# First norm of a two-layer diffusion backbone: modulation, norm and first products taken one input tile at a time

## The reference

```python
def rms(x):
    xf = x.astype(jnp.float32)
    return (xf * lax.rsqrt(jnp.mean(xf * xf, axis=-1, keepdims=True) + EPS)).astype(x.dtype)

def modulate(x, shift, scale):
    return rms(x) * (1 + scale[:, None]) + shift[:, None]
...
    mod = jax.nn.silu(c) @ p['w_ada'] + p['b_ada']
    mod_c = (jax.nn.silu(c_ctx) @ p['w_ada'] + p['b_ada'])[None]
    sh1, sc1, g1, sh2, sc2, g2 = jnp.split(mod, 6, axis=-1)
...
    h = modulate(x, sh1, sc1)
    hc = modulate(cx, csh1, csc1)
    z = h @ p['w_in']
```

## Time and profile before

| | us |
|---|---|
| median of 3 runs (lowest, highest) | 2370.47 (2367.01, 2371.37) |
| the profiled execution: its time | 2370.61 |
| its span in the profile | 2368.9 |
| PE busy | 2278.4 (96%) |
| DVE busy | 1348.6 (57%) |
| ACT busy | 937.4 (40%) |
| POOL busy | 164.8 (7%) |
| granted clock of PE, mean | 0.992 |

### The profile page before, as it was taken

The page is one execution under the profiler, slowest core; times in us unless marked ns, Lnnn a source line. Parts: engine busy times, 40 slices in busy tenths (PEclk is TensorE's granted clock), DMA queues, the critical chain, the costliest instruction groups (busy, mean ns, idle before and its releaser), DMA issues.

```text
span 2368.9 us, 35088 instructions
## 1 busy us (share of the span) xinstructions
PE 2278.4 (96%) x12916; PEld 1896.0 (80%) x12916; DVE 1348.6 (57%) x1954; ACT 937.4 (40%) x1381; POOL 164.8 (7%) x169
## 2 busy tenths in 40 slices
PE   6999988999999999999999999999999998999999
PEld 6788766788888878888888876776788878888887
DVE  6555566476667475425534566556745566645545
ACT  3454556522223243213312345546643334423332
POOL 2113010000000000000000002220100000000000
PEclk9999999999999999999999999999999999999999
DMA  7112110244343311111111131121045552222223
GB/s 284 45 54 72 36 40 19 72 156 138 133 142 133 124 54 62 62 63 63 62 62 63 62 117 63 63 71 32 36 144 176 175 178 78 101 98 92 94 98 115
DMA packets 58625, 221.26 MB, mean 93 GB/s; under 512 B 6720, under 2 KB 6720, under 8 KB 57872
## 3 DMA queue, kind: packets, MB, share of 16 engines
q1 hardware_dynamic: 44496, 160.46, 19.5%
q0 software_dynamic: 14016, 59.26, 7.1%
HBM read 214.45 MB, written 5.24 MB: 93 GB/s over the span
## 4 chain that ended last, share of the span: by engine, by line
PE 86%; DVE 6%; ACT 3%; issue 3%; DMA 1%; PEldq 0%; SPq 0%; PEld 0%; DVEq 0%; ACTq 0%
PE PS L611 83%; PE PS L903 3%; DVE TM L1459 1%; ACT W_hi L1081 1%; DVE XY L1459 1%; ACT TM L1081 1%; DVE H_lo L1459 1%; DVE ROPE L1512 1%; DVE W_lo L1456 1%; ACT XY L1081 1%; DVE F_lo L1456 1%; DMA ROPE<-w_mod 1%; ACT F_hi L1081 0%; DMA XY<-x_in 0%; ACT H_hi L1081 0%
## 5 line engine op out<-in xcount | busy, mean ns | idle before, releaser
L611 PE MATMUL PS<-H_hi,W_hi 128*128 128x512 f32 (+1 forms) x2256 | 689.3, 358 | 25.0 <-DVE H_lo L1459 9.6
L611 PE MATMUL PS<-H_hi,W_lo 128*128 128x512 f32 (+1 forms) x2256 | 678.7, 354 | 0.0
L611 PE MATMUL PS<-H_lo,W_hi 128*128 128x512 f32 (+1 forms) x2256 | 676.3, 353 | 0.0
L1456 DVE TENSOR_TENSOR W_lo<-W_st,W_hi 128x1024 fp32r<-128x1024 f32 x278 | 343.5, 1237 | 569.3 <-ACT W_hi L1081 567.8
L1081 ACT ACTIVATE W_hi<-W_st 128x1024 fp32r<-128x1024 f32 x278 | 293.7, 1057 | 838.8 <-PE PS L611 829.1
L611 PEld LDWEIGHTS PS<-H_hi,W_hi 128*128 128x128 f32 x2256 | 377.1, 189 | 102.9 <-issue 30.5
L611 PEld LDWEIGHTS PS<-H_lo,W_hi 128*128 128x128 f32 x2256 | 374.5, 189 | 61.3 <-issue 2.7
L611 PEld LDWEIGHTS PS<-H_hi,W_lo 128*128 128x128 f32 x2256 | 375.2, 189 | 59.1
L611 PE MATMUL PS<-F_hi,W_hi 128*128 128x512 f32 (+1 forms) x968 | 296.2, 355 | 13.5 <-DVE XY L1459 5.1
L611 PE MATMUL PS<-F_hi,W_lo 128*128 128x512 f32 (+1 forms) x968 | 295.3, 354 | 0.0
L611 PE MATMUL PS<-F_lo,W_hi 128*128 128x512 f32 (+1 forms) x968 | 293.3, 352 | 0.0
(11 more groups left out here) (129 smaller groups left out, 2086.9 us busy)
## 6 DMA issues: line engine op xcount, KB each, us to landing
W_st<-w_all SPq DMA_DIRECT2D x278, 512.0 KB, 3.5
RA<-w_mod POOLq DMA_DIRECT2D x40, 512.0 KB, 3.7
TM<-w_mod POOLq DMA_DIRECT2D x40, 512.0 KB, 3.7
RA<-w_ada SPq DMA_DIRECT2D x8, 512.0 KB, 8.7
XY<-bias_na POOLq DMA_DIRECT2D x2, 1792.0 KB, 7.3
RA<-w_mod SPq DMA_DIRECT2D x6, 512.0 KB, 8.2
XY<-x_in SPq DMA_DIRECT2D x4, 768.0 KB, 11.5
x_spill<-XY POOLq DMA_DIRECT2D x1, 3072.0 KB, 11.1
```

The source lines that it names most:

```text
L611: return nc.tensor.matmul(o, lhsT, rhs, start=start, stop=stop)
L1456: return nc.vector.tensor_tensor(o, a, b, f)
```

## The change

In layer 0 alone, the modulation, the norm and the first two output tiles of the input stage are interleaved over the eight input tiles.

- SP's order of loads is a list, FIRST_LOADS: scale and x first, W blocks 0 and 1 after x piece 2, the shift tiles from place 12 on.
- PE: the sum of squares is eight accumulated products of the squares with the matrix of 1/1024, over all 768 columns. The shift of tile j is a row: the conditioning columns are now stationary (128x2), the weight tile moves (128 columns, eight k). ACT copies the row (2x128) to SBUF, PE turns it into a column (128x2) by a product with a 2x2 identity, DVE adds the bias. Then, for each k, PE makes shift row k+2, shift column k+1, and the products of input tile k with W blocks 0 and 1.
- POOL's six additions go.
- ACT: six squares, both W_hi, two squares, the root over 768 columns, two copied rows, and per k the two pieces of H_hi and the copy of row k+2.
- DVE: scale sums 0 to 2, both W_lo, sums 3 and 4, the scale of five tiles, the Newton step over 768 columns, and per k the shift addition, both products, H_lo of tile k-1, and the scale sums of tile k+5 with its three small steps.
- The early tiles are inside PE's first_norm, ahead of its phase marks; `two_early_tiles` stays for the other norms.

```diff
+def first_norm_counts():
+
+    return dict(sq=KT, y0=1, y_sq=1, newton=2, norm_u=2 * KT, norm_hi=2 * KT, norm_lo=2 * KT)
+
+
+FIRST_LOADS = (("scale", 0), ("x", 0), ("scale", 1), ("x", 1), ("scale", 2), ("x", 2), ("w", 0), ("w", 1), ("x", 3),
+               ("scale", 3), ("scale", 4), ("shift", 0), ("shift", 1), ("shift", 2), ("scale", 5), ("shift", 3),
+               ("scale", 6), ("shift", 4), ("scale", 7), ("shift", 5), ("shift", 6), ("shift", 7))
+AHEAD = 5

...
-            for j in range(KT):
-                if j >= 3:
-                    sp.wait_ge(S["scale_acc"], 2 * (j - 2))
-                sp.dma_start(SCALE_W[j % 3], w_mod[SC1 + j]).then_inc(scale_loaded[j % 3], 16)
-                if j >= 3:
-                    sp.wait_ge(S["ada_used"], j - 2)
-                sp.dma_start(SHIFT_W[j % 3], w_ada[j]).then_inc(shift_loaded[j % 3], 16)
-                if j < KT // 2:
+            for what, j in FIRST_LOADS:
+                if what == "scale":
+                    if j >= 3:
+                        sp.wait_ge(S["scale_acc"], 2 * (j - 2))
+                    sp.dma_start(SCALE_W[j % 3], w_mod[SC1 + j]).then_inc(scale_loaded[j % 3], 16)
+                elif what == "shift":
+                    if j >= 3:
+                        sp.wait_ge(S["ada_used"], j - 2)
+                    sp.dma_start(SHIFT_W[j % 3], w_ada[j]).then_inc(shift_loaded[j % 3], 16)
+                elif what == "x":
                     k = 2 * T * j
                     sp.dma_start(XY[:, k:k + 2 * T], x_in[:, k:k + 2 * T]).then_inc(x_loaded[j], 16)
+                else:
+                    sp.dma_start(W_st[:, j, :], w_all[IN_BLOCKS[j]]).then_inc(w_loaded[j], 16)
             for l in range(DEPTH):
                 b0 = B_LAYER * l
                 for v, stored in enumerate(IN_BLOCKS):
-                    load(b0 + v, (b0 + v) % 2, B_LAYER_STORED * l + stored, first=b0 + v < 2)
+                    if b0 + v >= 2:
...
             pool.dma_start(PAR[:, :], par[0]).then_inc(S["par_loaded"], 16)
-            for k in range(1, KT - 1):
-                pool.wait_ge(S["sq"], k + 1)
-                wait(pool, "sq_sum", k - 1)
-                nc.gpsimd.tensor_tensor(TT, SQ[0] if k == 1 else TT, SQ[k % 2], ALU.add).then_inc(S["sq_sum"], 1)
             pool.wait_ge(S["scale_acc"], 2 * KT)
...
-            def ada_tile(o, w):
+            def shift_rows(j):
+
+                pe.wait_ge(shift_loaded[j % 3], 16 * (j // 3 + 1))
+                wait(pe, "sh_row", j - 1)
                 for k in range(KT):
-                    ins = mm(o, w[:, P * k:P * k + P], CC[:, k, :], k == 0, k == KT - 1)
-                return ins
-
-            def ada():
-
-                pe.wait_ge(S["silu_c"], 1)
-                for j in range(KT):
-                    pe.wait_ge(shift_loaded[j % 3], 16 * (j // 3 + 1))
-                    ada_tile(PS[:, 2 * j:2 * j + 2], SHIFT_W[j % 3]).then_inc(S["ada_used"], 1)
+                    ins = mm(bank(4 + j % 2)[0:2, 0:P], CC[:, k, :], SHIFT_W[j % 3][:, P * k:P * k + P], k == 0,
+                             k == KT - 1)
+                ins.then_inc(S["ada_used"], 1)
+
+            def shift_columns(j):
+
+                pe.wait_ge(S["sh_row"], j + 1)
+                pe.wait_ge(S["newton"], 1)
+                wait(pe, "sh_add", j - 1)
+                mm(bank(6 + j % 2)[:, 0:2], SH_ROW[j % 2], MT[0:2, M_ID, 0:2], True, True).then_inc(S["sh_tr"], 1)

...
             def first_norm():
-                pe.wait_ge(S["sq_sum"], KT - 2)
-                for h, (s0, sn) in enumerate(halves(T)):
-                    mm(stat_at(T, h), MT[:, M_ONE, :], TT[:, s0:s0 + sn], True, False)
-                pe.wait_ge(S["sq"], KT)
-                for h, (s0, sn) in enumerate(halves(T)):
-                    mm(stat_at(T, h), MT[:, M_ONE, :], SQ[1][:, s0:s0 + sn], False, True).then_inc(S["ss"], 1)
-                base.advance(**norm_counts(False))
+                pe.wait_ge(S["const_loaded"], 16)
+                for k in range(KT):
+                    pe.wait_ge(S["sq"], k + 1)
+                    for s0, sn in segs(T):
+                        ins = mm(pair(3)[:, s0:s0 + sn], MT[:, M_ONE, :], SQ[k % 2][:, s0:s0 + sn], k == 0, k == KT - 1)
+                    ins.then_inc(S["sq_pass"], 1)
+                pe.wait_ge(S["silu_c"], 1)
+                shift_rows(0)
+                shift_rows(1)
+                shift_columns(0)
+                for k in range(KT):
+                    if k + 2 < KT:
+                        shift_rows(k + 2)
+                    if k + 1 < KT:
+                        shift_columns(k + 1)
+                    for t in range(2):
+                        if k == 0:
+                            have_block(t)
+                        pe.wait_ge(S["norm_hi"], 2 * k + 2)
+                        pe.wait_ge(S["norm_lo"], 2 * k + 2)
+                        ins = gemm_k(t, T, t, k, KT, H_hi, H_lo)
+                        if k == KT - 1:
+                            ins.then_inc(S["block_done"], 1)
+                base.advance(**first_norm_counts())

...
-                    act.wait_ge(x_loaded[k // 2], 16)
-                    wait(act, "sq_sum", k - 1 if k >= 2 else 0)
-                    op(SQ[k % 2][:, 0:w], X3[:, k, 0:w], ACT.Square).then_inc(S["sq"], 1)
-                for b in range(2):
-                    split_hi(b, b, 16)
+            def square_of_x(k):
+                act.wait_ge(x_loaded[k // 2], 16)
+                wait(act, "sq_pass", k - 1)
+                op(SQ[k % 2], X3[:, k, :], ACT.Square).then_inc(S["sq"], 1)
+
+            def shift_row(j):
+                act.wait_ge(S["ada_used"], j + 1)
+                wait(act, "sh_tr", j - 1)
+                op(SH_ROW[j % 2], bank(4 + j % 2)[0:2, 0:P], ACT.Copy).then_inc(S["sh_row"], 1)

...
-            def first_norm(ph):
+            def first_norm():
+                for k in range(6):
+                    square_of_x(k)
+                for b in range(2):
+                    split_hi(b, b, 16)
+                for k in range(6, KT):
+                    square_of_x(k)
+                act.wait_ge(S["eps_set"], 1)
                 load_root_table()
-                begin(act, ph, "pe", "dve")
-                for h in range(2):
-                    root(T, h)
-                for h in range(2):
-                    for k in range(KT):
-                        high(T, h, k, SH1)
-                base.advance(**norm_counts(False))
+                act.wait_ge(S["sq_pass"], KT)
+                op(NY0, pair(3, T), ACT.Abs_reciprocal_sqrt, bias=EPSB).then_inc(S["y0"], 1)
+                act.wait_ge(S["y0"], 1)
+                op(NRT, NY0, ACT.Square).then_inc(S["y_sq"], 1)
+                shift_row(0)
+                shift_row(1)
+                for k in range(KT):
+                    for h, (s0, sn) in enumerate(halves(T)):
+                        act.wait_ge(S["norm_u"], 2 * k + h + 1)
+                        op(H_hi[:, k, s0:s0 + sn], NU[k % 3][:, s0:s0 + sn], ACT.Identity,
+                           bias=MOD[:, stream(s0), SH1 + k:SH1 + k + 1]).then_inc(S["norm_hi"], 1)
+                    if k + 2 < KT:
+                        shift_row(k + 2)
+                base.advance(**first_norm_counts())

...
+            def scale_sums(j):
+                dve.wait_ge(scale_loaded[j % 3], 16 * (j // 3 + 1))
+                for c in range(2):
+                    if j == 0:
+                        dve.wait_ge(S["cb_silu"], c + 1)
+                    wait(dve, "scale_acc", 2 * j + c)
+                    nc.vector.tensor_tensor_reduce(SCALE_P, SCALE_W[j % 3], CB[c], 1.0, 0.0, ALU.mult, ALU.add,
+                                                   MOD[:, c, SC1 + j:SC1 + j + 1]).then_inc(S["scale_acc"], 1)
+
+            def scales(j0, j1):
+
                 dve.wait_ge(S["adab_loaded"], 16)
-                dve.wait_ge(S["scale_acc"], 2 * KT)
-                dve.wait_ge(S["ada_used"], KT)
-                v = PS[:, 0:2 * KT].rearrange("p (j c) -> p c j", c=2)
+                dve.wait_ge(S["scale_acc"], 2 * j1)
                 for c in range(2):
-                    m = MOD[:, c, SC1:SC1 + KT]
-                    tt(m, m, ADAB[:, SC1:SC1 + KT], ALU.add).then_inc(S["mod_step"], 1)
-                    tt(MOD[:, c, SH1:SH1 + KT], v[:, c, :], ADAB[:, SH1:SH1 + KT], ALU.add
-                       ).then_inc(S["mod_step"], 1)
-                n_mod[0] += 4
+                    m = MOD[:, c, SC1 + j0:SC1 + j1]
+                    tt(m, m, ADAB[:, SC1 + j0:SC1 + j1], ALU.add).then_inc(S["mod_step"], 1)
+                n_mod[0] += 2
                 dve.wait_ge(S["mod_step"], n_mod[0])
+                m = MOD[:, :, SC1 + j0:SC1 + j1]
+                nc.vector.tensor_scalar(m, m, 1.0, -0.5, ALU.add, ALU.mult).then_inc(S["mod_step"], 1)
+                n_mod[0] += 1
+                dve.wait_ge(S["mod_step"], n_mod[0])
+
+            def shift(j):
+                dve.wait_ge(S["sh_tr"], j + 1)
```

(67 more changed lines are left out.)

41 lines of the change are left out of this document (10 added, 31 removed).

## The result

The changed kernel took 2384.3 us (median of 4, 2382.4 to 2390.5) against 2370.6 us: ratio 1.006 [1.0043, 1.0077], slower by 13.8 us. Two later comparisons of the same two kernels gave 1.0087 [1.0059, 1.0114] (+24.9 us) and 1.0094 [1.0079, 1.0110] (+21.6 us), so the first one was at the lower edge of what this kernel does.

The account below looks back on a forecast made before the run. PE, 96% busy, was taken to bound the kernel from tile 2's start at 75.17 us; that start 22.7 us later plus 1.9 for the clock gave +24.6 on 2370.6, so 2395.2 us, range 2380 to 2407.

Parts of the forecast that it names:

- DVE's loop earlier, part 1: Loads, squares and scale sums ahead of DVE's loop: it starts at 32.0 us against 51.16 before, 19 us earlier.
- The order in the queues, part 2: Loop over H tiles: in-order queues make DVE and PE alternate, with a period of 6.85 us fast, 10.4 us slow.
- Price of a row: PE's shift row of 16 passes in the loop: 1.9 us at the fast clock, 3.5 us at the slow.
- The clock: PE in the loop: idle 2.4 us per period lowers the clock in most, half the work at either level, period 8.6 us.
- X: End of both early tiles on PE: 93.6 us with mixed clock, 82.2 fast, 105.3 slow.
- Periods at 6.9 us with the clock at 1.00: Sign in the loop that would show the prediction's clock term to fail.
- so I expect a fall in most periods: PE in the loop: the clock falls in most periods and rises in each stretch of dense work.
- The rival of a slow clock in every step: Loop: products too short between waits to bring the clock back; X 105.3, mark +34.4, total 2407 us; chance 0.20.
- The hand-over, part 3: From X to tile 2 on PE: PE idle 4.3 us, tile 2 at 97.9, then 1.9 us for slow clock.
- What was costed at nothing: GpSimd additions gone, 9 small scale steps, 6 shift additions on DVE, POOL's ROPE load, W blocks 2 and 3: no cost.
- The faster rival: Loop: DVE not held by column k+2 and alone sets the pace; tile 2 at 66.3, total 2363.6 us; chance 0.07.
- Between mark and end: From PE's start of tile 2 to the kernel's end: 1.9 us added for slow clock after the idle time.

Follow-up runs that it names:

- e0: The changed kernel again, no edit, for a second sample: 2392.4 us, 1.0087 of the kernel before.
- e11: The changed kernel a third time, no edit, on another chip: 2393.6 us, 1.0094 of the kernel before.
- e1: The changed kernel with PE making shift row k+3 and column k+2 ahead of product k: 2369.6 us, 1.0001 of the kernel before.
- e4: The changed kernel with tile 1 three steps behind tile 0 and PE's phase marks ahead of tile 0's last step: 2389.3 us, 1.0086 of the kernel before.
- e7: The changed kernel with unused products in PE's gaps, 12 ahead of the first product, 6 ahead of each other: 2385.1 us, 1.0074 of the kernel before.
- e8: The changed kernel with row k+4 and column k+3 ahead of product k, e4's lag and marks, 14 unused products before the first: 2361.9 us, 0.9959 of kernel before.
- e12: The edit of e7 to the changed kernel again, on e11's chip: 2385.0 us, 1.0057 of the kernel before.
- e9: The changed kernel with all shift rows, columns and scale sums ahead of the first piece of H: 2370.0 us, 0.9998 of the kernel before.

## Why the prediction came out as it did

- **DVE's loop earlier, part 1: right.** Forecast 32.0, seen 30.94, in e0 31.75, in e11 32.78, so the 1 us is no more than the executions differ by. The squares ended at 25.7 us (forecast 26), the Newton steps took 2.0 (1.9). The scale sums ran at 1.23 us without POOL beside them, as reckoned from the earlier trace rows.
- **The order in the queues, part 2: right, and it is the cause.** Forecast period at the fast clock 6.85 us, seen 6.92 to 7.00. e1 undoes this one thing and the loss is gone.
- **Price of a row: right at both levels.** 1.91 us (forecast 1.9) and, wholly slow, 3.47 in e4 (3.5). But the two ends of the forecast were not two forms of load, they were the two clocks. At the slow level the old form, with 128 stationary columns, took 0.217 us a pass (48 in 10.40 us) and the new one, with 2, the same (16 in 3.47 us); at the fast level the new one took 0.12, and so did the transposes with 128. So the 1.00 that the window of 5 to 30 us shows for the kernel before does not fit its own passes. The Trainium skill's rule that a stationary load goes by its columns ("TensorE: Matmul & The Clock Gate", section "LDWEIGHTS (loading the stationary operand)") is borne out in direction alone: from 60 to 72 us of the changed kernel, at clock 1.00, a load of 2 columns is recorded with 85 ns and one of 128 with 188 (behind the bar: busy us, mean ns), and the time of a pass did not depend on it.

```profile
L623 PEld LDWEIGHTS PS<-RA,CC 128*2 128x2 f32 x32 | 2.6, 85 | 1.2 <-issue 0.5
L623 PEld LDWEIGHTS PS<-H_lo,W_hi 128*128 128x128 f32 x8 | 1.2, 188 | 0.2
```

- **The clock: the mechanism right, its size a matter of the execution.** This is the term that made 2395.2 out of 2382. I took 8.6 us for a period; in e0 three of the five with a row are 8.3 to 8.5 (one 9.57), in e11 four are 8.4 to 8.6; e0's tile 2 stands at 97.41 against 97.9 forecast. The execution that was profiled first had one slow period (9.11) and then four at 7 us, so X was 85.5 instead of 93.6 and tile 2 came 8.0 us sooner than forecast. "Periods at 6.9 us with the clock at 1.00" was the prediction's own sign that the clock term fails, and in that execution it did. The step that failed is "so I expect a fall in most periods": the row it rested on, 1.8 us of idle PE in two gaps within 3.4 us and a fall behind them, shows that gaps can lower the clock, not that they do each time. That the later medians, +24.9 and +21.6 us, stand so near the forecast +24.6 is in part luck, since the sum took nothing for what differs between executions behind tile 2.
- **The rival of a slow clock in every step** did not come: 10.4 us was the period of no run with single rows. In the first profile five of seven products behind a wait started at the fast level; in e0 three of seven did, so 2407 was too high. The Trainium skill, same page, section "HAM oscillation — how this bites in real kernels", describes a kernel whose every K tile starts cold behind a load wait of about 3 to 5 us. The waits here are of 2.5 us, shorter than those, and the traces show some starts slow and some fast.
- **The hand-over, part 3: right,** 4.34 us of idle PE at either clock (4.3 forecast); slow terms behind it for 3 to 5 us. 1.9 us was forecast for them, and 1.4 (e7) to 2.1 (e0) are seen: some four to seven terms at 0.64 instead of 0.35, five in the first profile (1.5 us).
- **What was costed at nothing was nothing:** the small scale steps and the shift additions lie inside DVE's waits of 1.8 to 4.7 us in the first profile, the removed additions on POOL were missed by none.
- **The faster rival** named the right condition, the stretch that DVE has to wait for, and its numbers hold once that condition is met: 66.3 us for tile 2 and 2363.6 were worked out, e8 has 67.55 and 2361.9. A step of DVE was put at 2.2 us and 5.3 with scale sums; e8 shows 2.19 and 5.26. e8 has the lag of tile 1 and the unused products as well, which that sum did not name, so how near the numbers come is in part luck.
- **Between mark and end** the sum took +1.9 us and nothing else. In the first comparison +14.7 at the mark was +11.9 in the span, although the slow terms behind it were there: 5.6 us were won back in a later stretch that the change does not touch, as below.

## What to carry to other kernels

When two engines with in-order queues feed each other, write down for each item what stands ahead of it in its own queue: an input for step k + 2 that is issued behind a product waiting for step k + 1 turns two overlapping loops into one that alternates. Here issuing the shift row and column one step earlier took back all of the 14 to 25 us, and two steps earlier, with a lag between the tiles, made it 0.4% faster than the old kernel. A dependency wait that idles PE for some 2.5 us in each period is to be priced twice, once as the wait and once as a clock that may fall in it; of two forecasts for the clock give both, and look at more than one execution before a size is believed.

## What the runs showed of the hardware that was not expected

**Equal gaps, unequal clock.** Gaps of 2.45 to 2.53 us between equal stretches of work kept 1.00 five times in a row in one execution and were followed by slow passes in four of six in another of the same program. Filling them with products that no one reads took the mean over 44 to 84 us from 0.83 (e11) to 1.00 (e12) and made the kernel 8.6 us faster. Less real work between the same gaps made e4 no faster that could be told. Why one gap lowers the clock and the next does not stays open.

**Two spacings of the same passes at one clock.** Behind some 470 us PE makes 1680 passes without a break, and from 500 to 600 us the granted clock is 1.00 in every execution. The chain of waits of the kernel before, and then that of the changed kernel's first profile:

```profile
474.04 297.05 PE PS L611 x1680
```

```profile
487.83 291.46 PE PS L623 x1680
```

The same passes took 5.6 us less. Of 14 profiled executions seven have 297.04 or 297.05 us here and seven 291.45 or 291.46, none lies between, and e0 (297.04) and e11 (291.46) are both the changed kernel. The rows of the timelines show where it lies: in the slower kind three terms of 768 columns take 1.06 us together, in the faster 1.04. It is not fixed for an execution either. In e8 one term starts at 58.45, 59.51 and 60.57 us, and then, behind a gap of 0.19 us at 61.98, another at 63.47, 64.51 and 65.55.

Other dense stretches show the same. An estimate from the starts of all passes behind 100 us (what those of the slower kind take above 1.04 us for three terms) gives 3.7 us in e4, the least, and 14.1 us in e9, the most; from tile 2 to the end of the span these two took 2289.0 and 2303.6 us, the shortest and the longest of all. e7 and e12 are one program, with tile 2 at 88.05 and 89.56 us; their profiled executions took 2380.2 and 2390.8 us, and the estimate is 5.8 and 12.8. So much of the spread between executions comes from this, and it hides a change of a few us unless medians are compared. What sets it was not found: no run was made for it, and it isn't the granted clock as recorded.
